# Down-projection products of a period in two gaps of four instead of three gaps of three, three and two

## What is computed

```python
D_MODEL, SEQ, DEPTH, N_MEM = 1024, 512, 2, 256
D_FF = 2816                       # 22 tiles of 128

def swiglu(x, wgu, wd):
    gate, up = jnp.split(x @ wgu, 2, axis=-1)
    return (jax.nn.silu(gate) * up) @ wd
...
    for i in range(DEPTH):
        h = h + 0.5 * swiglu(rms_norm(h, ffn1_norm[i]), ffn1_wgu[i], ffn1_wd[i])
        ...   # mixing stage: differential attention and a gated MLP, then w_out
        h = h + cross_attention(rms_norm(h, cross_norm[i]), rms_norm(mem, mem_norm[i]), ...)
        h = h + 0.5 * swiglu(rms_norm(h, ffn2_norm[i]), ffn2_wgu[i], ffn2_wd[i])
    return rms_norm(h, final_norm)
```

## Time and profile before

| | |
|---|---|
| time, median of 3 runs (lowest to highest) | 2100.28 us (2099.39 to 2100.61) |
| span of the profiled execution | 2098.5 us |
| TensorE busy | 2084.8 us, 99% |
| VectorE busy | 1645.2 us, 78% |
| ScalarE busy | 986.8 us, 47% |
| mean granted TensorE clock | 0.998 |

### The profile page before, as it was taken

How to read it: one execution, slowest core, us unless ns; L and a number is a source line. 1 busy time by engine, 2 the same in 40 slices (tenths; PEclk the granted TensorE clock), 3 DMA queues, 4 the chain that set the end, 5 groups by cost and what they waited for, 6 DMA issues and landing times.

```text
span 2098.5 us, 32639 instructions
## 1 busy us (share of the span) xinstructions
PE 2084.8 (99%) x13143; PEld 1867.3 (89%) x13143; DVE 1645.2 (78%) x2460; ACT 986.8 (47%) x1491; POOL 149.6 (7%) x114
## 2 busy tenths in 40 slices
PE   9999999999999999999999999999999999999998
PEld 7999998889888889999889999988898888999997
DVE  7998886658654789888799988766686458898885
ACT  6444444446433544444454444343464345444442
POOL 0000003100120300000110000030002111000001
PEclk9999999999999999999999999999999999999999
DMA  6333323323231343332233333243233224333321
GB/s 197 101 112 99 103 86 113 124 81 101 96 106 41 92 129 107 118 100 91 75 116 116 106 111 106 66 142 99 81 102 104 77 66 135 91 111 103 100 85 56
DMA packets 268018, 212.14 MB, mean 101 GB/s; under 512 B 7422, under 2 KB 234332, under 8 KB 267868
## 3 DMA queue, kind: packets, MB, share of 16 engines
q1 hardware_dynamic: 264608, 205.55, 31.5%
q10 hardware_dynamic: 3260, 4.51, 0.8%
HBM read 207.93 MB, written 2.10 MB: 100 GB/s over the span
## 4 chain that ended last, share of the span: by engine, by line
PE 98%; ACT 1%; issue 0%; DVE 0%; POOL 0%; POOLq 0%; DVEq 0%; ACTq 0%
PE ps L2004 21%; PE ps L2005 20%; PE ps L2006 20%; PE ps L2220 11%; PE ps L2222 11%; PE ps L2221 11%; PE ps L2493 1%; PE ps L2451 0%; PE ps L2371 0%; PE ps L2561 0%; PE ps L2298 0%; PE ps L2498 0%; PE ps L2025 0%; PE ps L2018 0%; PE ps L2047 0%
## 5 line engine op out<-in xcount | busy, mean ns | idle before, releaser
L2005 PE MATMUL ps<-hid_lo,wn_hi 128*128 128x512 f32 x640 | 251.7, 393 | 0.0
L2004 PE MATMUL ps<-hid_hi,wn_hi 128*128 128x512 f32 x640 | 251.5, 393 | 0.0
L2006 PE MATMUL ps<-hid_hi,wn_lo 128*128 128x512 f32 x640 | 249.0, 389 | 0.0
L1473 DVE SCALAR_TENSOR_TENSOR h<-ps,h 128x512 f32<-128x512 f32 x224 | 153.0, 685 | 31.3 <-PE ps L2006 31.0
L668 ACT ACTIVATE w_hi<-raw 128x2048 fp32r<-128x2048 f32 x61 | 116.8, 1915 | 123.6 <-PE ps L2006 91.4
L2220 PE MATMUL ps<-t_hi,form_hi 128*128 128x256 f32 x576 | 159.6, 277 | 0.0
L2222 PE MATMUL ps<-t_hi,form_lo 128*128 128x256 f32 x576 | 159.6, 277 | 0.0
L2220 PE MATMUL ps<-hn_hi,form_hi 128*128 128x256 f32 x576 | 159.5, 277 | 0.0
L2222 PE MATMUL ps<-hn_hi,form_lo 128*128 128x256 f32 x576 | 159.4, 277 | 0.0
L2222 PE MATMUL ps<-t_hi,more_lo 128*128 128x256 f32 x576 | 159.3, 277 | 0.0
L2221 PE MATMUL ps<-t_lo,form_hi 128*128 128x256 f32 x576 | 159.2, 276 | 0.0
(11 more groups left out here) (344 smaller groups left out, 5975.6 us busy)
## 6 DMA issues: line engine op xcount, KB each, us to landing
sraw<-in_ffn_wgu_dram SPq DMA_DIRECT2D x144, 512.0 KB, 4.9
raw<-in_ffn_wd_dram SPq DMA_DIRECT2D x48, 512.0 KB, 3.8
raw<-in_ffn_wd_dram SPq DMA_DIRECT2D x80, 256.0 KB, 4.1
raw<-in_w_in_dram SPq DMA_DIRECT2D x40, 512.0 KB, 4.4
raw<-in_cross_wkv_dram SPq DMA_DIRECT2D x32, 512.0 KB, 4.0
raw<-in_ffn_wgu_dram SPq DMA_DIRECT2D x30, 512.0 KB, 4.8
raw<-in_w_out_dram SPq DMA_DIRECT2D x16, 512.0 KB, 4.3
raw<-in_cross_wq_dram SPq DMA_DIRECT2D x16, 512.0 KB, 3.8
```

Source lines behind the costliest of these rows:

```text
L1473: dve.scalar_tensor_tensor(out=h[:, m, :], in0=ps[:, down_bank(c, m), :], scalar=0.5, in1=h[:, m, :], op0=ALU.mult, op1=ALU.add).then_inc( ...
L2004: pe.matmul(dst, a_hi, b_hi, start=start, stop=False)
L2005: pe.matmul(dst, a_hi, b_lo, start=False, stop=False)
L2006: return pe.matmul(dst, a_lo, b_hi, start=False, stop=stop)
```

## The change

The products of a period are divided over two gaps in place of three. From period 4 on, gaps 0 and 1 have four products each (before: three, three and two); in periods 1 to 3 both have two (before: two, one and one). `gap(n, 2)` is gone from TensorE's loop. On VectorE the additions that belonged to gap 2 go to where those of gap 1 stand, or, for periods 1 to 3, those of gap 1 now stand where those of gap 2 stood. The number of instructions of each kind stays the same. The changed kernel's lines behind the edits are up to three lower.

```diff
 def gap_products(n):
 
     if n == 0:
-        gaps = [[(0, 0), (1, 0)], [(0, 1), (1, 1)], []]
+        gaps = [[(0, 0), (1, 0)], [(0, 1), (1, 1)]]
     elif n < 4:
-        gaps = [[(2 * n, 0), (2 * n, 1)], [(2 * n + 1, 0)], [(2 * n + 1, 1)]]
+        gaps = [[(2 * n, 0), (2 * n, 1)], [(2 * n + 1, 0), (2 * n + 1, 1)]]
     else:
         i = 8 * ((n - 4) % 3)
-        gaps = [[divmod(i + a, 3) for a in range(*ab)] for ab in ((0, 3), (3, 6), (6, 8))]
+        gaps = [[divmod(i + a, 3) for a in range(*ab)] for ab in ((0, 4), (4, 8))]
     return (1 if n < 4 else 2 + (n - 4) // 3), gaps
...
                     if n >= 2:
                         hid_low(fast_tile(n - 2), G[:, n % 2, :])
-                    if n:
-                        add_gap(n - 1, 2)
+                    if 1 <= n - 1 < 4:
+                        add_gap(n - 1, 1)
...
                 fast_product_(FAST - 2)
                 hid_low(fast_tile(FAST - 2), G[:, FAST % 2, :])
-                add_gap(FAST - 1, 2)
                 up1(FAST - 1)
                 add_gap(FAST, 0)
                 add_gap(FAST, 1)
...
                 fast_product_(FAST - 1)
-                add_gap(FAST, 2)
                 down_split(CHUNKS - 1, 1)
...
                     gap(n, 1)
                     if n:
                         fast_step(n - 1, 5, 6)
-                    gap(n, 2)
                 last_chunk()
```

## The result

| | before | after |
|---|---|---|
| time, median of 5 runs (lowest to highest) | 2100.38 us (2099.39 to 2101.13) | 2110.50 us (2110.28 to 2111.41) |
| span of the profiled execution | 2098.5 us | 2108.4 us |
| mean granted TensorE clock | 0.998 | 0.998 |

The ratio is 1.0048, 95% interval 1.0038 to 1.0059: 10.1 us slower, where 8.6 us were forecast. The clock is the same, so the time went into the order.

A forecast was written before the change was run, and what follows sets the result against it. TensorE, busy 99% of the span, was taken to bound the kernel. Boundaries -3.0, period 4 +5.4, the tie +0.4 and the FFN's end +5.8 gave +8.6 on 2100.3, so 2108.9 us; 8-in-10 range 2103.2 to 2112.8.

The forecast's parts named there:

- What bounds the kernel: TensorE, busy 99% of the span, never waits inside the FFN loops, so any new wait adds to the time in full.
- Term 1: Fewer shape changes on TensorE: 56 gaps at 0.045 us and 12 at 0.035 us saved, 3.0 us gained.
- Term 2: Product (2, 0) in period 4 waits for down_split(c, 1) on DVE: 1.35 us in each of four FFNs, 5.4 us lost.
- Term 3: Product (2, 0) in periods 7, 10, 13 and 16 ties with its split: 0.03 us in each of 16 periods, 0.4 us.
- Term 4: End of an FFN: output tile 7's addition holds DVE's queue, making down_split(7, 1) late; 1.45 us each, 5.8 us lost.
- What costs nothing: Moving parts 2, 3, 5 and 6 makes no other wait late; the closest, gate0, keeps 1.5 to 2.1 us.
- Rule against row: The skill's fixed cost per matmul, none for shape changes, would give 2111.9 us; the prediction followed the profile's 0.13 us a period.
- (a): Rival: boundaries only, DVE not late at down_split(2, 1) or the FFN's end; 2097.3 us, faster; 5%.
- (b): Rival: only one of the two late places, period 4 or the FFN's end, is late; 2103.3 us; 13%.
- (e): Rival: the change does next to nothing, all its terms being smaller than read; 2100.3 us; 4%.
- (c): Rival: the tie in periods 7, 10, 13 and 16 falls late, 0.2 us more in each of 16; 2112.1 us; 12%.
- (d): Rival: the excess at boundaries belongs to something that stays, such as each new bank's first matmuls; 2111.9 us; 6%.

The follow-up runs named there:

- split_first: Changed kernel with down_split(c, 1) ahead of form_sums in periods 4, 7, 10, 13 and 16; 2103.25 us.
- four_gaps: Kernel before, with the third product of gap 0 put between parts 2 and 3 in periods 4 to 17, one boundary more each; 2102.36 us.
- one_gap_split_before_product: `split_before_product` with a single gap of eight products from period 4 on, additions as early as products allow, ScalarE's rounding ahead of copy_b; 2095.72 us.
- split_before_product: `split_first` plus output tile 7's addition back behind hidden tile 17's product, and down_split(7, 1) ahead of both; 2098.16 us.
- r0_three_gaps: Changed kernel, but periods 4, 7, 10, 13 and 16 keep three gaps of three, three and two products; 2105.06 us.

## Why the prediction was right, and where it was off

The prediction held in sign and size and in most of its mechanism: 2108.9 us forecast, 2110.5 measured. The lengths of the periods tell the terms apart. They are taken on the PE timeline from the first matmul of part 1 to the next one, in us, and are means over the four FFNs; r is the position in the chunk.

| kernel | periods 1 to 3 | 4 | 7, 10, 13, 16 (r = 0) | others from 5 to 15 |
|---|---|---|---|---|
| before | 12.33 | 15.08 | 15.10 | 15.10 |
| after | 12.34 | 16.52 | 15.15 | 15.05 |
| `split_first` | 12.34 | 15.05 | 15.05 | 15.05 |
| `four_gaps` | 12.33 | 15.36 | 15.12 | 15.12 |
| `one_gap_split_before_product` | 12.34 | 15.16 | 15.01 | 15.02 |

- **What bounds the kernel.** Right. Every wait of PE reached the end in full: `split_first` takes away 7.4 us of waits and slow steps by its periods, and gave 7.25 us.
- **Term 1, the boundaries, -3.0.** Right for the 56 gaps of periods 4 to 17: they are worth 0.047 us or a little more each, 2.7 us, where 0.045 was read. Wrong for the 12 gaps of periods 1 to 3: 0.035 each was taken without a row, and they gave nothing. Before, two gaps there were single products, and `four_gaps` shows such a gap at 0.02 us; two of them made into one of two products leave the cost as it was. With them the term is -2.7 by the rows. The step from two gaps to one has 0.035 to 0.045 us a period. `split_before_product` shows only -2.0 by the runs, as it has 0.5 us of slow steps of its own; the rest is no more than the 1 us or so over which runs of one kernel spread.
- **Term 2, period 4, +5.4.** Right: 1.35 us forecast, 1.37 measured, in each FFN. The work of 13.3 us on DVE and the 0.14 us from DVE to PE came out as 13.33 and 0.15. Left out was the restart, 0.08 us each. Together 5.9 us by the periods.
- **Term 3, the tie, +0.4.** It was a tie, and it fell to the late side: 0.09 us in each of 16 periods (15.15 against 15.05), 1.5 us, where 0.03 and 0.4 us were taken. This is the largest part of the miss, 1.1 us. The first step of (2, 0) has 0.06 to 0.07 of it; in period 7 the matmuls behind it, out of gap 1 and into part 5, are slower too.
- **Term 4, the last chunk, +5.8.** The size was right (1.31 + 0.11 = 1.42 against 1.45 an FFN), the reason only half, so the size had some luck. I put the wait down to the addition that holds the queue. The row has a second bound just under it, up0 behind part 6, which has eight products ahead of it in period 18 where it had six; with the addition back, 3.3 us stay. The addition alone is worth 2.35 us, and the split ahead of the product and the addition another 2.9.
- **The sum.** By the rows -2.7 + 5.9 + 1.5 + 5.8 = +10.5 us, beside +10.1 by the runs and +9.9 by the profiled spans. Against the forecast of 8.6, term 3 is 1.1 short, the restarts in term 2 are 0.5 and term 1 is 0.3.
- **What costs nothing.** gate0 never became late in the changed kernel, as worked out. In `r0_three_gaps` and `four_gaps`, where it has a product less, it did in period 4.
- **Rule against row.** The Trainium skill's fixed cost for each matmul ("TensorE: Matmul & The Clock Gate", section "Wait — 56ns, not 53.3ns?") would have given 2111.9 us, nearer to the measured time than mine, and for the wrong reason: periods with the same 108 matmuls take 15.12, 15.10, 15.05 and 15.01 us with four, three, two and one gap. The measurement decides against it.
- **The rivals.** (a), (b) and (e) are out, (c) came true to a third, (d) is out, as these periods have the same products, with the same first matmuls of a bank, and differ in length.

## What to carry to other kernels

When TensorE is busy throughout, moving its work has two prices: a small one per change of shape, here 0.02 us for a gap of one product and 0.04 to 0.05 for a longer one, and the spare time of whatever the moved instruction needs. Read the second from both timelines, producer's end against consumer's new start, at the first iteration and at the last, where the pipeline is not yet, or no longer, in step; here all the large waits were there. An addition that waits for TensorE belongs behind everything that TensorE itself waits for, and a repair is finished only when the bound just behind the repaired one has been read too. A difference of two run times is the price of one thing only when the periods show it nowhere else: half of the 2.0 us of `four_gaps` was a late gate0 in one period, and no list of waits named it.

## What was not expected of the hardware

A gap of one product is not a short version of a longer one: its three matmuls are slow, but the half-size ones behind it are not (0.11 us apart in `four_gaps`), so it costs 0.02 us where a gap of two or more has 0.04 to 0.05. After a wait TensorE's next step was slow as well: 0.31 us in period 4 and 0.34 in the last chunk where a step takes 0.23, in each of the eight waits, so a wait costs 0.1 us more than its own late step. With both it costs 0.24 to 0.27 us more than the idle time that the rows give (1.45 against 1.21 in period 4, 1.42 against 1.15 in the last chunk). And a tie of a few hundredths is not free: product (2, 0) in period 7 shows no idle time at all and yet a first step of 0.30 us, in a period 0.13 us too long.
